# An encoder block on eight cores: group maps scaled early into four buffers, a weight ring of 21, the norm row spread by matmul, the short row tile fourth, copies on one queue

## The reference

```
u = rms_norm(h, g_mix);  z = u @ w_in            # value, gate, pool, gate A, gate B: 1024 columns each
a = z_val * sigmoid(z_gate)                      # then a depthwise convolution over 31 tokens, + b_dw
y_conv = silu(layer_norm(a, ln_g, ln_b)) @ w_conv_out
m[g] = (window mean over 2, 4, 8 or 16 tokens - p) @ w_pool[g]     # four groups of 256 channels
y_pool = (m * pool_scale) @ w_pool_out
h = h + (sigmoid(zA) * y_conv + sigmoid(zB) * y_pool) @ w_o
v = rms_norm(h, g_ffn);  h = h + (silu(v @ w_gate) * (v @ w_up)) @ w_down
return rms_norm(h, g_final)                      # without the meta tokens
```

## Time and profile before

| what | value |
|---|---|
| median of three runs (lowest to highest) | 1066.98 us (1064.65 to 1275.44) |
| the profiled execution: its own time | 1064.49 us |
| its span on the slowest core (core 1); all cores | 1062.9 us; 1055.2 to 1062.9 |
| granted TensorE clock, mean of a core | 0.984 to 0.990 |
| PE busy | 1018.8 us (96%) |
| DVE, ACT, POOL busy | 427.8, 306.8, 176.1 us |
| DMA of POOL's queue (weights), SP's, ACT's | 42.6%, 11.6%, 2.1% of 16 engines |

### The profile page before, as it was taken

The page is one execution under the profiler, slowest core; times in us unless marked ns, Lnnn a source line. Parts: engine busy times, 40 slices in busy tenths (PEclk is TensorE's granted clock), DMA queues, the critical chain, the costliest instruction groups (busy, mean ns, idle before and its releaser), DMA issues.

```text
span 1062.9 us, 17032 instructions; the slowest of 8 cores (1055.2 to 1062.9 us)
## 1 busy us (share of the span) xinstructions
PE 1018.8 (96%) x5979; PEld 502.5 (47%) x5979; DVE 427.8 (40%) x628; ACT 306.8 (29%) x530; POOL 176.1 (17%) x329
## 2 busy tenths in 40 slices
PE   5799888999999999999999999999999999999996
PEld 2455444444444444444346555544445444444442
DVE  4264444762363222321144665685336212211133
ACT  4233334622233233321112333462114311111111
POOL 3311111111113221110213111201111311111011
PEclk9899999999999999999999999999999999999999
DMA  9798785264337865551548977525433854555032
GB/s 230 126 248 160 139 172 94 44 126 60 61 109 143 152 112 93 83 78 23 77 152 190 221 155 153 93 42 119 60 57 103 139 75 75 76 74 79 1 100 99
DMA packets 59523, 116.73 MB, mean 110 GB/s; under 512 B 9714, under 2 KB 9714, under 8 KB 59440
## 3 DMA queue, kind: packets, MB, share of 16 engines
q0 software_dynamic: 38592, 70.27, 42.6%
q1 hardware_dynamic: 18160, 36.70, 11.6%
q10 hardware_dynamic: 2688, 8.67, 2.1%
HBM read 160.24 MB, written 8.39 MB: 159 GB/s over the span
## 4 chain that ended last, share of the span: by engine, by line
PE 92%; DMA 5%; DVE 1%; issue 1%; ACT 0%; SPq 0%; DVEq 0%; POOLq 0%; POOL 0%; ACTq 0%
PE ps L374 86%; PE ps L499 5%; DMA h<-xe 2%; DMA wr<-wst 2%; DMA xt<-xe 1%; PE ps L406 1%; DVE s L534 0%; DVE acc_s L510 0%; DVE wps L559 0%; SPq L214 0%; ACT d_sb L503 0%; DVE ub L396 0%; DVEq L892 0%; ACT psb L524 0%; ACT uT L417 0%
## 5 line engine op out<-in xcount | busy, mean ns | idle before, releaser
L374 PE MATMUL ps<-vT,wr 128*128 128x512 bf16 x1408 | 306.4, 379 | 0.0
L374 PE MATMUL ps<-uT,wr 128*128 128x352 bf16 (+2 forms) x1664 | 294.5, 336 | 4.4 <-DMA wr<-wst 3.8
L214 POOL DMA_DIRECT2D wr<-wst x268 | 142.9, 536 | 715.0 <-PE ps L374 645.4
L374 PEld LDWEIGHTS ps<-uT,wr 128*128 128x128 bf16 x1664 | 162.9, 99 | 133.6 <-issue 16.9
L374 PEld LDWEIGHTS ps<-vT,wr 128*128 128x128 bf16 x1408 | 137.1, 98 | 162.6
L374 PE MATMUL ps<-wr,fT 128*128 128x512 bf16 x704 | 153.1, 379 | 3.0 <-DMA wr<-wst 3.0
L702 DVE TENSOR_TENSOR fT<-ps,sgf 128x512 bf16<-128x512 f32 x88 | 60.9, 692 | 221.4 <-PE ps L374 196.6
L701 ACT ACTIVATE sgf<-ps 128x512 f32<-128x512 f32 x88 | 52.5, 597 | 218.6 <-PE ps L374 218.6
L374 PEld LDWEIGHTS ps<-wr,fT 128*128 128x128 bf16 x704 | 68.5, 98 | 87.3 <-issue 5.5
L722 ACT ACTIVATE sqj<-h 128x512 bf16<-128x512 f32 x32 | 20.1, 629 | 137.8 <-DVE h L720 137.8
L499 PE MATMUL ps<-rep,wr 128*32 128x512 bf16 x1024 | 58.2, 380 | 0.0
(11 more groups left out here) (67 smaller groups left out, 662.6 us busy)
## 6 DMA issues: line engine op xcount, KB each, us to landing
wr<-wst POOLq DMA_DIRECT2D x268, 256.0 KB, 4.9
rep<-aT SPq DMA_DIRECT2D x248, 65.8 KB, 4.2
xt<-xe SPq DMA_DIRECT2D x24, 512.0 KB, 4.4
out<-h ACTq DMA_DIRECT2D x15, 512.0 KB, 2.7
h<-xe SPq DMA_DIRECT2D x8, 512.0 KB, 8.7
gb_s<-gb SPq DMA_DIRECT2D x3, 512.0 KB, 5.5
wpt<-wpt SPq DMA_DIRECT2D x4, 256.0 KB, 10.5
rep<-aT ACTq DMA_DIRECT2D x8, 65.8 KB, 7.8
```

The source lines that it names most:

```text
L214: e.dma_start(out=o[1], in_=o[2]).then_inc(o[3], 16)
L374: S.op(PE, lambda e: e.matmul(out, lhsT=lhsT, rhs=rhs, start=start, stop=stop), [lhsT, rhs], [out], signal=signal)
```

## The change

Six things are different. (1) wps has four buffers. The scalings are a step of their own, `wp_scale`: for groups 3 and 2 at the end of START (S0), for 1 and 0 after c0, and the loads of wpt for 1 and 0 go on SP right behind the first two scalings. (2) The step w0 stands before p1 and c7 and no longer after them; the order of the weight units follows. (3) The ring has 21 buffers. (4) The norm's row is loaded as one row of 1024 values (grow, 4 KB) ahead of everything, multiplied by a row of ones on TensorE in two fp32 matmuls of 512 columns, and copied by VectorE to all 128 partitions of gb; the 512 KB load of the spread-out row, between row tiles 1 and 2, is gone. (5) Row tile 8 is loaded right behind row tile 2, ahead of row tile 3, and the step L8 is gone. Ahead of the first transpose stand 4 + 4 idle matmuls, where 19 were. (6) All sixteen copies of the opening's im2col are issued on SP; before, eight of them were on ACT.

```diff
--- before.py
+++ after.py
@@ -31,20 +31,20 @@
 LN_EPS = 1e-5
 GRAN = 64
 PSUM_G0 = 10_000_000
-RING = 18
+RING = 21
 UNIT = 1024
 
 PC_BGA, PC_BGB, PC_BDW, PC_LNG, PC_LNB, PC_PSC = 0, 8, 16, 24, 32, 40
 PC_COLS = 48
 
 P1_STEPS = ["v0", "v1", "p6", "v2", "p7", "c0", "v3", "c1", "w3", "p4", "v4", "c2", "p5", "v5", "c3", "w2",
-            "p2", "v6", "c4", "v7", "c5", "p3", "w1", "p0", "c6", "p1", "c7", "w0"]
+            "p2", "v6", "c4", "v7", "c5", "p3", "w1", "p0", "c6", "w0", "p1", "c7"]
 P2_STEPS = ["G0", "G1", "P0", "P1", "G2", "P2", "G3", "Y0.0", "Y1.0", "Y2.0", "Y0.1", "Y1.1", "Y2.1", "P3", "Y3.0", "Y3.1"]
 for _c in range(4, KC):
     P2_STEPS += [f"G{_c}", f"P{_c}", f"Y{_c}.0", f"Y{_c}.1"]
-START = """L3 I19 A0 B0 T0 I4 L4 A1 E0d W1 B1 T1 I4 L5 A2 E1d W1 B2 T2 A3 E2d B3 G00 T3 L6 A4 E3a W1 B4 H00 T4 L7 A5 E4d W1 B5
-V00 G10 T5 L8 C0 A6 E5a W1 B6 H10 G01 T6 A7 E6d W1 B7 V10 H01 T7 A8 E7a V01 B8 G11 H11 T8 W2 E8d G02 H02 V11 V02 R0
-G12 H12 V12""".split()
+START = """L3 I4 A0 B0 T0 I4 L4 A1 E0d W1 B1 T1 I4 L5 A2 E1d W1 B2 T2 A3 E2d B3 G00 T3 L6 A4 E3a W1 B4 H00 T4 L7 A5 E4d W1 B5
+V00 G10 T5 C0 A6 E5a W1 B6 H10 G01 T6 A7 E6d W1 B7 V10 H01 T7 A8 E7a V01 B8 G11 H11 T8 W2 E8d G02 H02 V11 V02 R0
+G12 H12 V12 S0""".split()
 
 
 def unit_order():
@@ -285,7 +285,7 @@
     aT = [m1.get(f"aT{i}", [128, EXTP], BF16) for i in range(3)]
     rep = [m1.get(f"rep{i}", [128, 4, EXTP], BF16) for i in range(2)]
     wpt = [m1.get(f"wpt{i}", [128, 512], F32) for i in range(2)]
-    wps = [m1.get(f"wps{i}", [128, 512], BF16) for i in range(2)]
+    wps = [m1.get(f"wps{i}", [128, 512], BF16) for i in range(4)]
     s1 = m1.get("s1", [128, EXTP], F32)
     s2 = m1.get("s2", [128, EXTP], F32)
     psb = m1.get("psb", [128, EXTP], F32)
@@ -471,14 +471,14 @@
     def vg_block(c, bi):
         vg_evict(c, bi, vg_mm(c, bi))
 
-    def im2col(c, two=False):
+    def im2col(c):
         st = c % 2
         tot = rep_sem[st].count + 16 * 16
         for s_ in range(4):
             for j in range(4):
                 o = rep[st][32 * s_:32 * s_ + 32, j, 0:REPW]
                 i_ = aT[c % 3][32 * j:32 * j + 32, s_:s_ + REPW]
-                S.dma((SP, ACT)[s_ % 2] if two else SP, rep_sem[st], o, i_, val=tot)
+                S.dma(SP, rep_sem[st], o, i_, val=tot)
 
     def vg_done(c):
         rel(2)
@@ -552,19 +552,19 @@
     def wp_load(g):
         S.dma(SP, wpt_sem[g % 2], wpt[g % 2][:], wp_d.ap()[g])
 
+    def wp_scale(g):
+        for k in range(2):
+            so, si, sc = wps[g][:, k * 256:(k + 1) * 256], wpt[g % 2][:, k * 256:(k + 1) * 256], pcc(PC_PSC, 2 * g + k)
+            S.op(DVE, lambda e, so=so, si=si, sc=sc: e.tensor_scalar(out=so, in0=si, scalar1=sc, scalar2=None, op0=ALU.mult),
+                 [si, sc], [so])
+
     def wpool(g):
         rows = [take(f"pr{2 * g + k}") for k in range(2)]
-        for k in range(2):
-            so, si, sc = wps[g % 2][:, k * 256:(k + 1) * 256], wpt[g % 2][:, k * 256:(k + 1) * 256], pcc(PC_PSC, 2 * g + k)
-            S.op(DVE, lambda e, so=so, si=si, sc=sc: e.tensor_scalar(out=so, in0=si, scalar1=sc, scalar2=None, op0=ALU.mult),
-                 [si, sc], [so])
-        if g >= 2:
-            wp_load(g - 2)
         for cc in range(2):
             for h in range(2):
                 bw = nb()
                 for k in range(2):
-                    mm(psum[bw][:], wps[g % 2][:, k * 256 + cc * 128:k * 256 + cc * 128 + 128],
+                    mm(psum[bw][:], wps[g][:, k * 256 + cc * 128:k * 256 + cc * 128 + 128],
                        rows[k][:, h * 512:(h + 1) * 512], k == 0, k == 1, k == 1)
                 wo_, wi = wpf[:, 2 * g + cc, h * 512:(h + 1) * 512], psum[bw][:]
                 S.op(ACT, lambda e, wo_=wo_, wi=wi: e.activation(out=wo_, in_=wi, func=AF.Copy), [wi], [wo_])
@@ -756,11 +756,14 @@
 
 
     zt = alloc_at("zt", [128, 512], BF16, f_start)
+    grow = alloc_at("grow", [1, D], F32, f_start + 1024)
+    g_sem = Prod(sem("d_grow"), 16)
+    S.dma(SP, g_sem, grow[:], gb_d.ap()[0:1, 0:D])
     s0_load(0, 0)
     S.dma(SP, cst[0], ident[:], id_d.ap())
     s0_load(0, 1)
-    S.dma(SP, gb_sem[0], gb[:, 0, :], gb_d.ap()[:, 0:D])
     s0_load(0, 2)
+    s0_load(0, 8)
     S.op(POOL, lambda e: e.memset(zt[:], 0.0), [], [zt[:]])
     S.op(POOL, lambda e: e.memset(nhalf[:], -0.5), [], [nhalf[:]])
     S.op(POOL, lambda e: e.memset(ones[:], 1.0), [], [ones[:]])
@@ -774,6 +777,12 @@
         for j in range(k):
             mm(psum[b_][:], zt[:, 0:128], zt[:], True, True, j == k - 1)
 
+    idle_mm(4)
+    for h in range(2):
+        b_ = nb()
+        g_i, g_p, g_o = grow[:, h * 512:(h + 1) * 512], psum[b_][:], gb[:, 0, h * 512:(h + 1) * 512]
+        mm(g_p, ones[0:1, :], g_i, True, True, True)
+        S.op(DVE, lambda e, g_o=g_o, g_p=g_p: e.tensor_copy(out=g_o, in_=g_p), [g_p], [g_o])
     rs0 = {}
 
     def row_a(k):
@@ -803,6 +812,11 @@
             S.dma(SP, cst[1], pc[:], pc_d.ap())
             wp_load(3)
             wp_load(2)
+        elif st[0] == "S":
+            wp_scale(3)
+            wp_scale(2)
+            wp_load(1)
+            wp_load(0)
         elif st[0] == "W":
             prefetch(k)
         elif st[0] == "G":
@@ -814,7 +828,7 @@
         elif st[0] == "I":
             idle_mm(int(st[1:]))
         elif st[0] == "R":
-            im2col(k, True)
+            im2col(k)
         elif st[0] == "E":
             row_e(k, DVE if st[2] == "d" else ACT)
         else:
@@ -827,7 +841,11 @@
             rel(2)
         else:
             run_p1(i, P1_STEPS[:2])
-        run_p1(i, P1_STEPS[2:])
+        for st in P1_STEPS[2:]:
+            run_p1(i, [st])
+            if i == 0 and st == "c0":
+                wp_scale(1)
+                wp_scale(0)
         if i == 0:
             S.dma(SP, cst[2], invc[:], ic_d.ap())
             S.dma(SP, gb_sem[1], gb[:, 1, :], gb_d.ap()[:, D:2 * D])
```

## The result

The changed kernel takes **1050.26 us** (median of four runs; those compared lie between 1049.86 and 1050.45), the kernel before, run beside it, 1066.11. The ratio is **0.9855, 95% interval 0.9832 to 0.9877**: 1.5% faster, where I had forecast 2.4% and 1041 us. The gain is clear of zero but under the 2% that this measurement tells from no change, an outcome to which I had given 0.19. The time lies 0.26 us above the upper end of my range. (ring_only, norm_full and best2 ran on a chip whose cores 4 to 7 were at a lower granted clock in most runs, with the kernel before too, so for these three I compare the slowest of cores 0 to 3, in the median 1062.6 us for the kernel before there.)

A forecast was written before the change was run, and what follows sets the result against it. TensorE, busy for 1018.8 of 1062.9 us, bounds the kernel; only its gaps and low-clock stretches can be won. 1064.5 - 23.2 - 3.7 + 1.3 + 1.0 = 1039.9, plus 1 for the median: 1041 us, range with rivals 1030 to 1050.

The forecast's parts named there:

- the copies' term: Opening's sixteen copies all on SP: c0's and c1's copies land about when due, 1 us more, bounds 0 and 4.
- rival (b): Copies for c0, c1 and some later convolution land late, TensorE waits 4 us twice or so: 1047 to 1050; chance 0.10.
- The short tile: Opening: row tile 8 loaded early holds tile 3 up by 9.0 us; first matmul of the last block 1.3 us later.
- The maps: First pass's mixing stage: waits on wps and clock loss go, 112.5 us against 135.7, 23.2 us less.
- Rival (c): Waits only change their name: VectorE's lag returns as waits for a PSUM bank or a sum, about 1060; chance 0.06.
- rival (d): SP's issues bound the stage, overtaking the old one at 0.98 us each; at 1.25 us about 1099; chance 0.04.
- The ring: Changes of down halves: with 21 tiles, ten instead of seven are loaded ahead, 3.7 us less.
- The norm row: Opening: one row replaces the 512 KB load; tile 2 lands earlier, -1.9 us, and +0.5 for one more issue.

The follow-up runs named there:

- ring_only: The kernel before with only the ring raised to 21 tiles: ratio 0.9996 (0.9976 to 1.0017) against the kernel before.
- norm_full: The changed kernel with the whole 512 KB norm load again between row tiles 1 and 2, no spreading: 0.9911 against the kernel before.
- best2: The changed kernel with 32 rows for tile 8, processed behind tile 3, wpt loads behind c1's copies, c0's copies on two queues: 0.9764 against the kernel before.
- wpt_behind: The changed kernel with the wpt loads of groups 1 and 0 behind c1's copies, their scalings behind c1: 0.9814 against the kernel before.
- ring18: The changed kernel with the ring of 18 tiles: 0.9914 (0.9896 to 0.9932) against the kernel before.
- short_last: The changed kernel with row tile 8 (31 rows) loaded last again, behind tile 7: 0.9831 against the kernel before.
- copies_two: The changed kernel with c0's sixteen copies on two queues again, eight on SP and eight on ScalarE: 0.9835 against the kernel before.

## Why the prediction was wrong, step by step

**The step that failed is the copies' term.** It said: issued at 24.7 us after the block, landed at 30.4, c1 due at 30.0, "I take 1 us more, bounds 0 and 4". Issue and due time came within 0.5 and 1.2 us of the forecast (25.2 and 31.2, the latter with c0's wait in it); the landing did not. I charged the two wpt loads with 1 us of issuing and took the median landing of a stretch in which no such load stood ahead. wpt_behind shows that median, 5.7, to be right without them and 9.2 right with them. That it is their place in SP's queue rather than bytes ahead on any queue is made likely by ring18 and not shown by a clean run. I also counted no half clock behind the wait. The term is 1.02 + 4.02 + 1.68 = 6.7 us and not 1, which is 5.7 of the 10.3 us missing. My rival (b), late copies at c0 and c1 partly at the lower clock, 1047 to 1050, is nearest to what happened, with one long wait and not two; I gave it 0.10. Its reason was the busy DMA engines. What I held against it, that the second pass keeps its pace at a DMA share of 0.87, said nothing on order in one queue, and nothing like these two loads stands there.

**The short tile** was sized too small, by little: 10.4 us at tile 3 and not 9.0, and from its square to its transpose 4.5 and not 3.8 us. The rest of that chain, 11.56 to tile 7 and 5.0 to the block, is near the forecast (12.2, 5.0). In sum 1.5 us too late. The part ahead of the price was right: without the early tile the square stands at 12.75 in short_last, where 14.05 - 1.9 + 0.5 = 12.65 was worked out.

**The maps** were right: no wait on wps, and 113.0 and 112.9 us for the stage without copies' waits and half clock, in two kernels, where 112.5 was forecast. Rival (c) is refuted by that, rival (d) by issues of 0.59 us in the middle. (Rival (d)'s 0.98 us is where the whole kernel would break even; by its own sum the stage is overtaken at 0.96.)

**The ring** was right in mechanism and size: 3.5 us by the traces, 3.7 forecast. **The norm row** moved tile 3 by 1.6 us, where 1.4 was forecast. **c7's wait** in the second pass, 2.29 us on core 0, was not forecast; it differs by core and stood on other cores before; its cause stays open.

## What to carry to other kernels

Price a transfer by what stands ahead of it in its queue, in bytes and not only in issues: a landing time read from a stretch without such a load is the lower end (here 5.7 us, and 9.2 behind 0.5 MB). When loads are moved earlier, ask which transfer with a due time they now stand in front of. And before a load's place is chosen, look at its row count: here 31 rows cost 10 us at the next tile, or 15 us of landing at the end, and 32 rows 0.7 us at the next tile (13.42 against 12.75).

## What the hardware showed that was not expected

Two loads of 256 KB ahead in the same queue went with some 3.5 us more for the landing of the sixteen copies behind (5.7 to 9.2 us in the middle on core 0; 5.5 to 5.7 and 8.3 to 9.4 over eight cores), at the same share of the DMA engines (1.12 and 1.11). One row more in a load of 31 brought the next 512 KB tile 9.7 us earlier. A wait of 4.02 us cost another 1.68 at the half level of the clock, and so did one of 2.04 us in copies_two on core 4; but the waits of 1.73 us in copies_two on core 0 and of 3.46 us on core 3 of the changed kernel were followed by c1 at full clock: the length of a gap alone does not tell whether the clock falls.
